# A hybrid decoder step: gated-delta chunks started inside the convolution, with 16x16 diagonal blocks inverted on VectorE

## The reference

```
G = cumsum(g); decay = exp(G_i - G_j) for i >= j
A = (beta k) k^T * decay, strictly lower
u, w = (A + I)^-1 [beta v, beta k exp(G)]
v_new = u - w S
o = (q exp(G)) S + (q k^T * decay) v_new
S_new = S exp(G_last) + (k exp(G_last - G))^T v_new
```

## Time and profile before

| what | value |
|---|---|
| median of 3 runs | 1606.65 us (1603.29 to 1607.93) |
| the profiled execution | 1601.89 us, its span 1600.1 us |
| mean granted TensorE clock | 0.974 |
| PE busy | 1475.9 us, 92% of the span |
| DVE busy | 559.6 us (35%) |
| ACT busy | 226.4 us (14%) |
| POOL busy | 149.3 us (9%) |
| DMA | 478.78 MB, mean 299 GB/s |

### The profile page before, as it was taken

One profiled execution on the slowest core, in us unless ns is written; L12 is line 12 of the kernel. 1 busy time (PEld: TensorE's weight loads), 2 busy tenths in 40 slices (PEclk: granted clock), 3 DMA queues, 4 the chain that ended last, 5 costly groups with the idle time before them and its releaser, 6 DMA issues.

```text
span 1600.1 us, 18873 instructions
## 1 busy us (share of the span) xinstructions
PE 1475.9 (92%) x7689; PEld 739.2 (46%) x7689; DVE 559.6 (35%) x1147; ACT 226.4 (14%) x443; POOL 149.3 (9%) x125
## 2 busy tenths in 40 slices
PE   6989999989887997999999999999999999999996
PEld 5874488779875754333333233223233323323322
DVE  2551560534555322364232232232223223224214
ACT  3113212122210011101011011011010011011002
POOL 0012011022400000100000010010010010010000
PEclk9999999999999997999999999999999999999999
DMA  5443335630023892999999999999999999999992
GB/s 200 157 158 108 124 132 173 207 133 2 1 68 115 304 374 77 390 411 418 416 417 417 416 416 417 418 415 418 417 415 418 417 416 417 418 416 417 417 416 81
DMA packets 121321, 478.78 MB, mean 299 GB/s; under 512 B 9691, under 2 KB 27835, under 8 KB 88299
## 3 DMA queue, kind: packets, MB, share of 16 engines
q1 hardware_dynamic: 121142, 477.27, 75.3%
q0 software_dynamic: 96, 0.33, 0.1%
HBM read 466.92 MB, written 10.85 MB: 299 GB/s over the span
## 4 chain that ended last, share of the span: by engine, by line
PE 49%; DMA 39%; DVE 5%; SPq 4%; ACT 1%; issue 1%; POOL 0%; DVEq 0%; ACTq 0%; POOLq 0%
DMA gus<-in_w_gate_up 37%; PE bank L1026 11%; PE bank L662 7%; PE bank L599 5%; PE bank L1045 4%; SPq L501 4%; PE bank L628 4%; PE bank L1004 2%; PE bank L962 2%; PE bank L1070 2%; PE bank L883 1%; PE bank L824 1%; PE bank L840 1%; DMA Ssg<-in_state_gdn 1%; PE bank L782 1%; DVE Ssg L1799 1%
## 5 line engine op out<-in xcount | busy, mean ns | idle before, releaser
L1026 PE MATMUL bank<-gus,xT 128*64 128x512 f32 x2048 | 460.7, 596 | 40.6 <-DMA gus<-in_w_gate_up 38.2
L1026 PEld LDWEIGHTS bank<-gus,xT 128*64 128x64 f32 x2048 | 140.4, 137 | 355.1 <-issue 239.5
L1942 DVE TENSOR_TENSOR glu<-bank,bgb 128x512 f32<-128x512 f32 x32 | 22.1, 691 | 654.0 <-issue 376.4
L1045 PE MATMUL bank<-dns,acT 128*64 128x512 f32 x1024 | 228.9, 600 | 0.0
L1045 PEld LDWEIGHTS bank<-dns,acT 128*64 128x64 f32 x1024 | 71.2, 138 | 136.5 <-issue 136.5
L1468 POOL PARTITION_BROADCAST bgb<-bgu x32 | 41.5, 1298 | 967.3 <-DMA bgu<-in_b_gate_up 855.1
L1965 DVE TENSOR_TENSOR X<-X,bank 128x512 f32<-128x512 f32 (+1 forms) x198 | 120.9, 673 | 16.1 <-PE bank L1070 13.0
L662 PE MATMUL bank<-HT,wslot 128*128 128x264 f32 x512 | 116.6, 388 | 0.6 <-ACT sq L1199 0.6
L662 PEld LDWEIGHTS bank<-HT,wslot 128*128 128x128 f32 x512 | 96.6, 190 | 18.1 <-issue 1.3
L1004 PE MATMUL bank<-hrow,O 128*64 128x512 f32 (+1 forms) x384 | 95.9, 617 | 4.4 <-DVE O L1925 4.4
L1070 PE MATMUL bank<-yb,CT 64*128 64x512 f32 (+1 forms) x384 | 94.5, 608 | 1.7 <-ACT CT L1335 1.6
(11 more groups left out here) (358 smaller groups left out, 1304.9 us busy)
## 6 DMA issues: line engine op xcount, KB each, us to landing
gus<-in_w_gate_up SPq DMA_DIRECT2D x256, 1024.0 KB, 20.5
dns<-in_w_down SPq DMA_DIRECT2D x128, 1024.0 KB, 22.1
wslot<-in_w_in SPq DMA_DIRECT2D x18, 2048.0 KB, 7.8
Ssr<-in_state_ret SPq DMA_DIRECT2D x4, 1024.0 KB, 8.3
out<-Ssr SPq DMA_DIRECT2D x4, 1024.0 KB, 6.7
wslot<-in_w_branch_a SPq DMA_DIRECT2D x2, 2048.0 KB, 8.4
wslot<-in_w_branch_b SPq DMA_DIRECT2D x2, 2048.0 KB, 10.1
out<-Ssg SPq DMA_DIRECT2D x8, 512.0 KB, 5.4
```

The lines of the kernel that those rows point to most:

```text
L1026: t = pe.matmul(B[part][64 * g:64 * g + 64, :], block_of(xT, k), gus[k][:, D * part + 512 * g:D * part + 512 * g + 512], start=(k == 0), s ...
L1045: t = pe.matmul(B[2][64 * g:64 * g + 64, :], block_of(acT, k), dns[4 * u + k // 2][:, k % 2, 512 * g:512 * g + 512], start=(k == 0), stop= ...
```

## The change

The first two thirds of the layer are put in another order; the experts are not touched.

- **The gates.** The cumulated g and beta (`GBc`) are transposed, copied to SBUF (`GT`), written to HBM and read back broadcast to all partitions (`Gb`, 2 MB), all during the convolution. The broadcasts by POOL and the products on them are gone.
- **The convolution's order.** k blocks first, then q, then v. The L2 norms, k k^T and the decay factors of both chunks lie between convolution blocks. The norm is exp(-0.5 ln x) on ScalarE instead of square root and reciprocal, here and in the later norms.
- **The base.** The 16x16 diagonal blocks of A (8 blocks, 8 heads, 2 chunks = 128 of them) are written by 16 DMAs to HBM and read back so that each block is one partition (`E`). VectorE inverts all 128 at once by 15 substitution steps of two small instructions (`base_step`), giving `UE` and its transpose `TE`. They go to HBM and come back by 32 DMAs into the diagonal blocks of `T` and `U`.
- **The levels.** Levels 4, 5 and 6 remain (blocks of 16, 32, 64), for both chunks together.
- **Fillers.** Feature blocks (z and g first) lie between the steps of the chunks and of the decoding state. The retention columns by tokens come after that, then retention as before among the last 16 features, then all 16 branch products in a row, b first. `Ssr`, the retention state of the decoding tokens, is loaded after `Ssg` is written out.

Core of the diff (`conv(a, b)` are convolution blocks, `squares_of` the sums for an L2 norm):

```diff
+WCOL = (4096, 4608, 3072, 3584, 5120, 5632, 6144, 6656, 2048, 2560, 0, 512, 1024, 1536, 7184, 7696, 8208, 8720)
+NBASE = 16
@@ sync @@
+            AC.wait(sp, "GT")
+            sp.dma_start(gates_out.rearrange("c r i -> r c i"), GT[:, :, :]).then_inc(s_gb, 16)
+            sp.wait_ge(s_gb, 16)
+            sp.dma_start(Gb[:, :, :, :].rearrange("p c r i -> p (c r i)"),
...
+            DV.wait(sp, "At1.1")
+            for b in range(KT):
+                rows = slice(NBASE * b, NBASE * b + NBASE)
+                for c in range(2):
+                    sp.dma_start(base_in[b, GH * c:GH * c + GH].rearrange("h j i -> j h i"), Gb[rows, c, GH:2 * GH, rows]
+                                 ).then_inc(s_e, 16)
+            sp.wait_ge(s_e, 256)
+            sp.dma_start(E[:, :, :], base_in.rearrange("b c j i -> (b c) j i")).then_inc(s_e, 16)
+            sp.wait_ge(s_ct, 20)
+            load_w(6)
+            DV.wait(sp, "UE")
...
+            sp.wait_ge(s_e, 304)
+            PL.wait(sp, "z")
+            for f, g in ((T, base_T), (U, base_U)):
+                for b in range(KT):
...
+            sp.wait_ge(s_ct, 24)
+            load_w(7)
@@ tensor @@
+            conv(5, 13)
+            PL.wait(pe, "sqk")
+            pe.wait_ge(s_hTev, 1)
+            for q in range(4):
+                squares_of(q, B[2 + q], GH, f"l2k{q}")
+            conv(13, 18)
...
+            pe.wait_ge(s_raw, CCH + 2)
+            pe.wait_ge(s_abev, 1)
+            DV.wait(pe, "At1.1")
+            AC.wait(pe, "lq3")
+            for t2 in range(CCH):
+                t = pe.transpose(B[2 + t2 // 4][0:11, P * (t2 % 4):P * (t2 % 4) + P], edges[:, t2, :], ident)
+            t.then_inc(s_eT, 1)
+            features(0, 2)
+            P0, P1, P2 = B[2:4], B[4:6], B[6:8]
+            pe.wait_ge(s_eTev, 1)
+            DV.wait(pe, "nq3")
...
+            features(2, 3)
+            pe.wait_ge(s_tu, 512)
...
+            for lv in (4, 5, 6):
...
@@ vector @@
+            def base_step(j):
+                n = NBASE - 1 - j
+                t = tE[:, 0:j + 1, 0:n]
+                link(v.tensor_tensor(t, bc(UE[:, 0:j + 1, j], n, 2), bc(E[:, j, j + 1:NBASE], j + 1, 1), ALU.mult))
+                f = UE[:, 0:j + 1, j + 1:NBASE]
+                return v.tensor_tensor(f, f, t, ALU.subtract)
...
+            taps(19, 22)
+            dve.wait_ge(s_e, 272)
+            for j in range(6):
+                link(base_step(j))
+            taps(22, 23)
+            for j in range(6, NBASE - 2):
+                link(base_step(j))
+            DV.did(base_step(NBASE - 2), "UE")
+            DV.wait(dve, "UE")
+            DV.did(v.tensor_copy(TE[:, :, :], UE[:, :, :].rearrange("p a i -> p i a")), "TE")
+            taps(23, 24)
+            for q in range(4):
+                l2norm(q, 0, "q")
+            dve.wait_ge(s_eT, 1)
+            for i in range(6):
+                t = v.tensor_copy(ctok[:, 512 * i:512 * i + 512], B[2 + i][0:11, :])
+            t.then_inc(s_eTev, 1)
```

More of the change, by code:

```diff
@@ new lines, in feature, with features @@
+            def feature(n):
+                u, m = n // 4 % 2, n % 4
+                if m == 0:
+                    pe.wait_ge(s_w[u], 16 * (n // 8 + (4 if n < 16 else 6)))
+                if n >= 2:
+                    pe.wait_ge(s_fev, n - 1)
+                for k in range(KT):
+                    t = pe.matmul(B[n % 2][:, 0:TOK], wslot[u][:, k, P * m:P * m + P], HT[:, k, :],
+                                  start=(k == 0), stop=(k == KT - 1))
+                t.then_inc(s_fm, 1)
+            def features(first, last):
+                for n in range(first, last):
+                    feature(n)
@@ new lines, in squares_of @@
+            def squares_of(q, bank, first, name):
+                MM.did(pe.matmul(bank[:, :], ones, sq[:, first + 2 * q:first + 2 * q + 2, :].rearrange("p h n -> p (h n)"),
+                                 start=True, stop=True), name)
+            conv(0, 2)
+            pe.wait_ge(s_gv, 2)
+            for c in range(2):
+                t = pe.matmul(B[7][:, GH * c:GH * c + GH], inc, gl[:, c, :], start=True, stop=True)
+            MM.did(t, "G")
+            conv(2, 4)
+            DV.wait(pe, "GB")
@@ L612, in _ @@
+            conv(20, 21)
+            for q in range(2, 4):
+                AC.wait(pe, f"lq{q - 2}")
+                squares_of(q, B[q], 0, f"l2q{q}")
+            conv(21, 24)
+            pe.wait_ge(s_raw, CCH + 2)
+            pe.wait_ge(s_abev, 1)
+            DV.wait(pe, "At1.1")
+            AC.wait(pe, "lq3")
             for t2 in range(CCH):
@@ new lines, in _ @@
+            sS = slice(2 * P, TOK)
+            AC.wait(pe, "sq1.0")
+            norm_sums(0)
+            DV.wait(pe, "S1.1")
+            DV.wait(pe, "nd")
+            for n, first in (("k", GH), ("v", 2 * GH)):
+                for h in range(GH):
+                    j, f = h % 4, P * (h // 4) + (2 * P if n == "v" else 0)
+                    t = pe.matmul(B[4][32 * j:32 * j + NB, f:f + P], uT[:, first + h, sS], ident, start=True, stop=True)
+                MS.did(t, n)
+            features(8, 9)
@@ new lines, in _ @@
+            AC.wait(pe, "sq1.1")
+            AS.wait(pe, "ln1.0")
+            norm_sums(1)
+            features(9, 10)
+            PS.wait(pe, "qkp")
+            DS.wait(pe, "z")
+            pe.wait_ge(s_sgl, 16)
+            for half_of, m in ((0, kmg), (2, qmg)):
+                for i in range(2):
+                    for b in range(NB):
+                        for j in range(4):
+                            t = pe.matmul(B[6][32 * j:32 * j + NB, P * (half_of + i):P * (half_of + i) + P],
+                                          m[:, 4 * i + j, b, :], Ssg[:, b, 4 * i + j, :],
+                                          start=(b == 0), stop=(b == NB - 1))
@@ new lines, in _ @@
+            features(10, 11)
+            DS.wait(pe, "o4")
+            for i in range(2):
+                t = pe.transpose(B[7][:, P * i + P:P * i + 2 * P], q4[:, i, :], ident)
+            MS.did(t, "o4T")
+            features(11, 12)
+            decode_state_g(0)
+            features(12, 13)
+            AS.wait(pe, "oqd")
+            MS.did(pe.matmul(B[7][:, 3 * P:3 * P + GH * NB], ones, oqd[:, :, :].rearrange("p h b -> p (h b)"),
+                             start=True, stop=True), "nd")
@@ new lines, in _ @@
+            l2norm(2, GH, "k")
+            l2norm(3, GH, "k")
+            taps(15, 19)
+            for c in range(2):
+                MM.wait(dve, f"KK1.{c}")
+                PL.wait(dve, f"dB.{c}")
+                At = Gb[:, c, GH:2 * GH, :]
+                halves(lambda i: f"At{i}.{c}", lambda i: v.tensor_tensor(
+                    half(At, i), half(At, i), quad(B[4 + 2 * c + i]), ALU.mult))
+            link(v.memset(UE[:, :, :].rearrange("p a i -> p (a i)")[:, 0:NBASE * NBASE:NBASE + 1], 1.0))
@@ new lines, in _ @@
+            keys(0, B[6:8])
+            level("U", 6, 0, B[2:4])
+            level("U", 6, 1, B[4:6])
+            values(0, B[6:8])
+            keys(1, B[2:4])
+            values(1, B[6:8])
+            for i in range(2):
+                MM.wait(dve, f"dS{i}.0")
+                DV.did(v.tensor_copy(half(Sg, i), quad(B[4 + i])), f"S{i}.0")
+            outputs(0, B[6:8])
+            AC.wait(dve, "rd")
+            for first, scale in ((0, P ** -0.5), (GH, 1.0)):
+                x = uT[:, first:first + GH, 2 * P:TOK]
+                t = v.scalar_tensor_tensor(x, sqd[:, first:first + GH, :], scale, x, ALU.mult, ALU.mult)
@@ L1814, in _ @@
+            for m in range(2 * KT):
                 branch_out(m)
```

1337 lines of the change are left out of this document (659 added, 678 removed).

## The result

The changed kernel took 1538.34 us (median of 4 runs, 1531.13 to 1540.82), the kernel before 1605.12 us beside it (4 runs, 1603.29 to 1607.93): a ratio of 0.9575, 95% interval 0.9538 to 0.9612. Run again in a later set it gave 0.958 (0.9551 to 0.9609). The forecast was 1540, range 1522 to 1566. The profiled execution took 1537.03 us, its span is 1535.2.

The account below looks back on a forecast made before the run. The experts' weight stream, 971 us, starts when TensorE reaches expert 0, so the first part's gain passes on in full. 87.0 us off, 20.8 added, net 66: profiled 1536, median 1540, range 1522 to 1566.

Parts of the forecast that it names:

- The levels, 39.4: Chunks' inverse: 22 groups of eight float32 products go, at 1.79 us each, saving 39.4 us.
- The chunks' waits, 21.1: TensorE's 21.1 us of waits in the chunks go, if fillers cover what takes their place.
- The base, 7.7 forecast: Inverting the diagonal blocks: TensorE stalls 6.7 us for arm (a) and 1.0 for arm (b), together 7.7.
- arm (b): Base: 32 scatters at 0.45 us plus landing, done at 47.4 us; TensorE waits 1.0 before the first Y.
- arm (a): Base: VectorE's taps, norms and `ctok`, done at 38.6 us; TensorE waits 6.7 before q k^T.
- The k norm's stall: Convolution after block 10: ScalarE's and POOL's 9.7 us against TensorE's 7.1, a stall of 2.6 us.
- The third slot: Retention: `Ssr` stands ahead of the third slot's load, which lands 3.9 us late, with 1 of clock.
- Slow clock: TensorE slower behind waits: 10.8 us taken off; 1.5 added at the base and 1 at the third slot.
- Dear small transfers: Rival, base: small DMAs cost 0.96 us an issue, 24 us more, all bare, giving 1564; chance 0.2.
- One after the other: Rival, base: each small DMA takes its 2.3 us to landing before the next, giving 1629; chance 0.04.
- VectorE binds the convolution: Rival, convolution: VectorE and ScalarE bind, POOL's work holding VectorE; 15 us on top, giving 1555; chance 0.12.
- The change buys nothing: Rival, whole kernel: the weight stream would set the end by itself; chance 0.02.

Follow-up runs that it names:

- b2r: Changed kernel with level 4 of the inverse left out for both chunks (outputs not the reference's): 1529.68 us, ratio 0.9522 to the kernel before.
- b4r: Changed kernel with the first eight feature blocks all behind chunk 1's last product, no fillers inside the chunks: 1544.00 us, ratio 0.962.
- c4: Changed kernel with one feature block moved from behind q k^T to ahead of it: 1540.66 us, ratio 0.9593.
- a1: Changed kernel with 32 more scatters of the same size, to dead tiles, awaited before the first Y: 1552.76 us, ratio 0.9685.
- b3r: Changed kernel with ScalarE's SiLU of k ahead of the two decay exponentials: 1535.07 us, ratio 0.9555.
- c3: Changed kernel with the 32 scatters merged into 16 and one feature block moved ahead of q k^T: 1530.65 us, ratio 0.9536.
- a3: Changed kernel with two later feature blocks moved ahead, one before q k^T, one before the first Y: 1542.34 us, ratio 0.9621.
- c2: Changed kernel with merged scatters, feature ahead of q k^T, third slot ahead of Ssr, Ssg in parts, SiLU of k first: 1516.86 us, ratio 0.9448.
- b1r: Changed kernel with Ssg loaded in three parts, each as soon as its place is dead: 1528.51 us, ratio 0.9517.
- c0: The changed kernel again, unaltered, in a later set: 1538.08 us, ratio 0.958.

## Why the prediction was right

**What bounds it, and what is passed on.** Held. The experts kept their 971 to 973 us, and the first part's gain reached the end but for the 2.2 us between `w_out` and expert 0. Over all the traces that stretch takes 68.0 to 71.4 us for the same instructions; it depends on how much of the expert gather behind VectorE's `O` runs at slow clock. Here TensorE works 26.3 us at a granted clock of 0.50 in the changed kernel (527.3 to 561.5) and 19.0 in the kernel before (595.9 to 623.2), which costs it 3.7 us more, while it waits 1.2 less for `O`. The forecast had no term for it.

**The levels, 39.4.** Held: rows of two groups every 3.57 us, and 1.79 a group in b2r.

**The chunks' waits, 21.1.** Gone, as forecast. The reason given was only half right: "if fillers cover what takes their place". Fillers cover 10.9 us at the base; in the levels, and nearly so behind them, none is needed (b4r). More than half of the 21.1 us was never in the levels or behind them. In the kernel before, TensorE waited twice for the masked copy of level 0, until 357.09 and until 412.92 us:

```profile
PE bank L811 <- DVE U L1708: 11.1, 2, 5.9
```

That copy's place is taken by the base, with 17.7 us of waits, 10.9 of them covered. That it is the other chunk which covers the copies inside the levels is argued from the order of the products: no run has the chunks one after the other on the new base.

**The base, 7.7 forecast, 6.8 measured.** Counted from the end of convolution block 18 (106.1 us; ScalarE's copy of it starts at 106.26), the first Y was to start at 47.4 and started at 47.6. Two errors cancel. The way to the scatters was shorter: they began at 28.3, forecast 30.7, because `E` landed 15.6 in and VectorE, still at its tap 21, never waited for it. The 32 scatters took 17.9 us at 0.56, forecast 14.4 at 0.45. The split was off too: 6.7 and 1.0 forecast, 3.8 and 3.0 measured, for `ctok` was ready 3 us earlier than reckoned. c4 shows that the split has no meaning of its own: arm (b) alone fixed the first Y, and the price named for arm (a) was not to be won by covering it. The 1.5 us of company in arm (a) came from a mean of 1437 ns over four instructions that took from 678 to 2810. That arm (b)'s cover is used up, and that each small DMA more is on the end, a1 shows at 0.5 us each.

**Small terms.** The k norm's stall: 2.6 forecast, 2.2 measured (the cause shown by b3r). `Ssg`: 7.3 forecast, 6.8. The third slot: 3.9 forecast, 3.4. `bv` and `kbG`: 1.3 forecast, 0.6 measured. Decoding copies 1.2, as forecast, though the profile names nothing that ended this wait; the last `Ssg` state 0.6, forecast 0.7. The L2 sums of the kernel before took 6.6 and 6.04 us (191.52 to 197.56), not 6.6 twice.

**Slow clock was the mis-sized term.** I took 1.5 us for the base, 1 behind the third slot and nothing elsewhere. Measured: 1.7 behind the k stall, 1.7 at q k^T, 2.1 at `Ssg`, 2.8 at the slot, 8.3 against 2.5. Each is the difference of the row behind the wait to its twin at full clock; the granted clock agrees, 0.50 (1.2 GHz, the lower of its two levels) in four stretches (76.77 to 80.19, 141.63 to 145.04, 237.20 to 244.03 and 312.29 to 319.12 us) in which TensorE works 16.7 us, so 8.4 of cost. The waits themselves came out 3 us lower than forecast in sum (2.2, 6.8, 6.8, 3.4 and 0.6 against 2.6, 7.7, 7.3, 3.9 and 1.3), so the added part was 3 us dearer than reckoned, and yet the stretch to `w_out` fell by 68.15, not 66.

Some 5 us more went away than I took off. Most of it is the slow clock of the kernel before, of which I had measured 4.8 and taken 6 more. Its trace has seven stretches behind the start of the convolution with a granted clock of 0.50, at 118.06, 356.99, 411.61, 449.15, 469.63, 486.70 and 544.73 us, 34.1 us in all. TensorE works 28.2 us in them. In the first, 6.0 us of work made the row 3.0 dearer; at that rate, half the work, they cost 14.1 us and not 10.8, so 3.3 more. Its waits at the decoding tokens' retention state fell from 1.8 and 1.2 us to one of 2.2, and the forecast had no term for them: 0.8. The last microsecond or so stays open.

The total came within 2 us of the forecast because these misses run against each other: 5 us more gone and 3 less of waits, against 6 more of slow clock and 2.2 behind `w_out`. The mechanism held; the closeness is luck.

**The rivals.** Dear small transfers: 0.47 and 0.56 us, far from 0.96. One after the other: the 32 scatters took 17.9 us where a chain of their landings (1.8 us each in the table of DMA issues) would take 58. The Trainium skill's DMA: Bandwidth & Descriptors (Anatomy of one DMA — SWDGE (gpsimd) path) puts a fixed cost of about 2.0 us on a DMA that GpSimd issues. The DMAs here are issued by SP; their trace has nearly the same for the landing of one (1.8 us for 8 KB, 2.1 for `E`'s 128 KB). It also shows that these costs overlap in a queue, so that the issue counts. VectorE binds the convolution: its taps became slower (below), but TensorE has no recurring stall between convolution blocks. The change buys nothing: refuted by the result.

## What to carry to other kernels

When two waits stand one behind the other, ask which event fixes the later start; the other wait is only cover that isn't needed, and covering it moves idle time without shortening it, until the binding one is moved (c4 against c3). When waits inside a stage disappear, ask which of them the new order covers and which belonged to a step that is gone. A filler needs its own weights loaded at the new place, so read the DMA queue's order, not only the engine's (a3). A wait costs more than its idle time: here up to 0.8 us of slow clock per microsecond waited, so the small waits, each cheap to remove, were worth 24 us together.

## What the runs showed of the hardware

**VectorE behind GpSimd.** An instruction of 8 columns took 7.73 us in the changed kernel and 9.31 in c3, where 24 columns took 0.18 in the kernel before. VectorE's timeline of c3, then GpSimd's:

```profile
145.60 0.69 DVE L1711 TENSOR_TENSOR Gb<-Gb,bank 128x512 f32<-128x512 f32 x1 [0.21 <-PE bank L598]
146.20 9.31 DVE L1738 TENSOR_TENSOR beG<-beta,eG 128x8 f32<-128x8 f32 x1
155.54 2.48 DVE L1717 TENSOR_TENSOR T<-T,bank 128x512 f32<-128x512 f32 x4
```

```profile
143.90 4.67 POOL L1479 TENSOR_TENSOR Al<-Gb,K 128x1024 f32<-128x1024 f32 x2
148.53 4.65 POOL L1479 TENSOR_TENSOR Gb<-Gb,K 128x1024 f32<-128x1024 f32 x2
153.15 2.34 POOL L1529 TENSOR_TENSOR qe<-qe,uT 128x1024 f32<-128x1024 f32 x1
155.45 0.39 POOL L1532 TENSOR_TENSOR sqd<-uT 128x128 f32<-128x128 f32 x1
```

`beG` reads two operands from SBUF. It ends just as GpSimd's run of five long instructions does, at 155.5, while the instructions before it, with one operand in PSUM, took their usual 0.69 beside the same run. The Trainium skill's SBUF — State Buffer (SBUF: two separate sides) has a shared port that one of the two engines holds for its whole instruction, where the other reads two SBUF inputs; the trace agrees, and adds that the small instruction got no turn between GpSimd's back-to-back ones. In the changed kernel this lay under TensorE's wait. In c3 and c2 it costs 1.3 us, VectorE's first subtraction of T being late. The taps read two SBUF operands as well. Beside GpSimd's two masks of 109.93 to 114.65 us a set of three took 3.50 us, the next set 1.52, and over all 72 the mean is 594 ns against 484 before. No run takes GpSimd's work away, so how much of these 110 ns is its doing isn't measured.

```profile
112.48 3.50 DVE L1627 SCALAR_TENSOR_TENSOR uT<-raw,cw,uT 128x256 f32<-128x256 f32 x3
...
116.28 1.52 DVE L1627 SCALAR_TENSOR_TENSOR uT<-raw,cw,uT 128x256 f32<-128x256 f32 x3
```

```profile
L1627 DVE SCALAR_TENSOR_TENSOR uT<-raw,cw,uT 128x256 f32<-128x256 f32 x72 | 42.8, 594 | 2.6
```

**A small DMA has one price.** 8 KB in 128 pieces of 64 bytes and 16 KB in 256 cost SP the same 0.47 to 0.62 us and landed 1.8 and about 2.0 us later. Between these two sizes, what counts is the number of DMAs; no run has larger ones of such pieces.

**The same wait, another bill.** Behind the same 2.2 us stall of k the same eight instructions took 5.40 us in the changed kernel and 3.70 in a3 and b1r; in those two, the convolution was 0.8 us longer ahead of it (its first 32 products took 9.6 us against 8.8, at a granted clock of 0.50 until 26.6 and 26.8 us against 25.6). Behind the wait of 3.3 to 3.6 us for the third slot the same 32 took 14.00 us in c3, 15.70 in c0 and 17.02 in a3. The granted clock falls behind a wait, but not always at the same instruction, and not behind every wait.
